# Router logits from x itself, x turned once into the output banks, the norm weight put on at the column copies, and two row products of a pair moved round the turns

## The reference

```python
x = x + m                                     # after the mixer
h = _rmsnorm(x, norm_ffn_g)                   # x * rsqrt(mean(x*x) + EPS) * norm_ffn_g
gp = softmax(ht @ w_router_group)             # 4 groups, the best one is taken
el = (ht @ w_router_expert)[its group]        # 8 experts of it
ep = softmax(el); tv, ti = lax.top_k(ep, 2); tv = tv / sum(tv)
for e in range(32):                           # D_MODEL 1024, EXPERT_FF 512
    a = silu(ht @ w_expert_gate[e]) * (ht @ w_expert_up[e])
    out = out + combine[:, e:e + 1] * (a @ w_expert_down[e])
y = _rmsnorm(x + out, norm_final_g)
```

## Time and profile before

| | us |
|---|---|
| median of 3 runs | 806.62 (805.08 to 806.87) |
| the profiled execution | 806.2 |
| its span | 804.2 |
| PE busy | 773.9 (96%) |
| DVE, ACT, POOL busy | 234.4, 176.4, 97.2 |
| chain that ended last: PE, DMA | 81%, 13% of the span |

### The profile page before, as it was taken

The page is one execution under the profiler, slowest core; times in us unless marked ns, Lnnn a source line. Parts: engine busy times, 40 slices in busy tenths (PEclk is TensorE's granted clock), DMA queues, the critical chain, the costliest instruction groups (busy, mean ns, idle before and its releaser), DMA issues.

```text
span 804.2 us, 10140 instructions
## 1 busy us (share of the span) xinstructions
PE 773.9 (96%) x4170; PEld 445.8 (55%) x4170; DVE 234.4 (29%) x533; ACT 176.4 (22%) x321; POOL 97.2 (12%) x128
## 2 busy tenths in 40 slices
PE   8999999999999999999999999999999989999995
PEld 7888887888888888863333333333333333333331
DVE  4099869482550322441101110111011101101112
ACT  3104333657544101231111001100110010010011
POOL 5300064523300000001101000001000000000001
PEclk9999999999999999999999999999999999999998
DMA  9845586578849974499999999999999999999993
GB/s 329 244 149 187 164 239 207 181 214 169 276 148 365 398 259 191 162 360 430 423 429 417 426 429 425 429 426 427 427 429 427 430 427 429 425 428 419 421 409 149
DMA packets 76374, 267.90 MB, mean 333 GB/s; under 512 B 5598, under 2 KB 37578, under 8 KB 63647
## 3 DMA queue, kind: packets, MB, share of 16 engines
q1 hardware_dynamic: 74402, 264.13, 84.3%
q10 hardware_dynamic: 1461, 1.45, 0.6%
q0 software_dynamic: 464, 1.64, 0.5%
HBM read 259.13 MB, written 8.55 MB: 333 GB/s over the span
## 4 chain that ended last, share of the span: by engine, by line
PE 81%; DMA 13%; DVE 2%; issue 1%; ACT 1%; POOL 1%; SPq 0%; DVEq 0%
PE bank L2007 23%; PE bank L1630 23%; PE bank L2045 10%; PE bank L1903 7%; PE bank L2053 6%; DMA slots<-in_w_expert_gate_dram 5%; DMA x_early<-in_w_expert_gate_dram 5%; DMA slots<-in_w_expert_down_dram 2%; PE bank L1850 2%; PE bank L1740 1%; DMA slots<-in_w_in_dram 1%; PE bank L2034 1%; DVE x_early L1488 1%; PE bank L1971 1%; PE bank L1662 1%
## 5 line engine op out<-in xcount | busy, mean ns | idle before, releaser
L1630 PE MATMUL bank<-hT,slots 128*128 128x264 f32 x832 | 189.6, 387 | 0.0
L2007 PE MATMUL bank<-slots,hT 128*64 128x512 f32 x624 | 177.9, 601 | 2.1 <-DMA slots<-in_w_expert_gate_dram 2.1
L1630 PEld LDWEIGHTS bank<-hT,slots 128*128 128x128 f32 x832 | 156.6, 190 | 26.8 <-issue 0.6
L1488 DVE TENSOR_TENSOR x_early<-x_early,bank 128x512 f32<-128x512 f32 x16 | 11.0, 688 | 376.6 <-PE bank L2007 376.6
L2007 PEld LDWEIGHTS bank<-slots,hT 128*64 128x64 f32 x624 | 55.1, 138 | 91.1 <-issue 86.5
L2045 PE MATMUL bank<-slots,wrep 128*64 128x512 f32 x304 | 85.4, 595 | 4.7 <-ACT wrep L1053 4.0
L2007 PE MATMUL bank<-slot,hT 128*64 128x512 f32 x208 | 81.4, 593 | 0.0
L793 POOL COPY hT<-x_early 128x512 f32 x30 | 17.9, 623 | 369.3 <-PE bank L2007 286.2
L2053 PE MATMUL bank<-hT,diag 128*128 128x512 f32 x128 | 59.2, 605 | 0.2 <-ACT hT L1065 0.2
L2045 PEld LDWEIGHTS bank<-slots,wrep 128*64 128x64 f32 x304 | 26.0, 137 | 49.3 <-issue 39.6
L1228 DVE SCALAR_TENSOR_TENSOR slot<-slot,rows_buf 128x256 f32<-128x256 f32 x120 | 49.4, 488 | 0.0
(11 more groups left out here) (301 smaller groups left out, 759.6 us busy)
## 6 DMA issues: line engine op xcount, KB each, us to landing
slots<-in_w_expert_gate_dram SPq DMA_DIRECT2D x15, 2048.0 KB, 23.2
slots<-in_w_expert_up_dram SPq DMA_DIRECT2D x15, 2048.0 KB, 28.7
slots<-in_w_expert_down_dram SPq DMA_DIRECT2D x15, 2048.0 KB, 29.7
slots<-in_w_in_dram SPq DMA_DIRECT2D x13, 2048.0 KB, 10.0
slots<-in_w_expert_gate_dram SPq DMA_DIRECT2D x10, 1024.0 KB, 26.2
slot<-in_w_expert_gate_dram SPq DMA_DIRECT2D x5, 2048.0 KB, 27.7
slot<-in_w_expert_up_dram SPq DMA_DIRECT2D x5, 2048.0 KB, 23.7
slot<-in_w_expert_down_dram SPq DMA_DIRECT2D x5, 2048.0 KB, 34.1
```

The costliest lines, as they stand in the source:

```text
L1488: dve.tensor_tensor(act.rearrange("s (f c) -> s f c", f=FT), act.rearrange("s (f c) -> s f c", f=FT), bank[UP][:, :].rearrange("s (c f) -> ...
L1630: last = mm(out, w[:, a, t * P:(t + 1) * P], (hT if c else xgain)[:, a, :], start=(a == 0), stop=(a == KT - 1))
L2007: last = mm(out[sl, :], xe[:, a, sl], expert_view(p, kind, e, a // 2)[:, a % 2, :], start=(a == 0), stop=(a == KT - 1))
```

## The change

It has five parts, all after the mixer's last projection but for the first line.

1. **Logits of x.** The router weights are multiplied once by `norm_ffn_g` on DVE, ahead of the wo groups, and `route` reads `xT`. The eight products into `hT` (L1407) are gone, and so are the copy of `hT` to DRAM (`h_rows`, L591) and the waits for it. The branch for experts with over 64 tokens, which this input does not enter, is rewritten to use `tok_rows`.
2. **x turned once.** `seat` now uses the transpose mode, and all four seats stand ahead of the ranking. ACT makes `xrow` from the output banks; only the eight sample rows are still turned into the `misc` banks. The sum of squares is made with 128 moving columns for each token tile, not one.
3. **Norm weight at the copies.** `xrow` now is x times `rs`. The weight is put on where columns are copied: DVE (`first_columns`) makes the first pair's `xe` from the gathered banks, in place of ACT, and POOL multiplies the later pairs' columns by it (L793 was a copy). A small load brings the weight.
4. **The choice** uses the engine's eight-largest operation (`dve.max`) and combined compare-and-multiply operations.
5. **Loads and row products.** SP issues half 18 ahead of `tok_rows`, and 19 ahead of 17. From the fifth pair on, two of the four row products of the pair before leave `combine_prompt` and stand one ahead of `turn(p)` and one behind it; a new semaphore `m_rows` makes ACT's copy to `ytok` and DVE's `weigh` wait for them.

```diff
@@ sync: loads @@
-                if c == WO + 1:
-                    sp.wait_ge(xg_ready, KT)
-                    sp.dma_start(h_rows[:, :, :], hT[:, :, :]).then_inc(h_stored, 16)
                 sp.wait_ge(proj.ready, proj.written(stream[c][1]))
                 load_slot(n)
+                if n == 5:
+                    sp.dma_start(g_by, ins["norm_ffn_g"][0].rearrange("(p a) -> p a", p=P)).then_inc(g_by_in, 16)
             load_half(16)
-            sp.wait_ge(*misc.read(("ht", 5)))
...
-            sp.wait_ge(seated, 1)
+            sp.wait_ge(misc.ready, misc.written(("ht", 5)))
             sp.wait_ge(x_kept, 1)
             load_half(18)
+            sp.wait_ge(row_made, 4)
+            sp.dma_start(tok_rows[0:SEQ, :].rearrange("(t p) d -> p t d", p=P), xrow[:, 0:2, :]).then_inc(rows_kept, 16)
...
@@ gpsimd: columns of pair p @@
-                    pool.tensor_copy(xe[:, :, e * SLOTS:(e + 1) * SLOTS], xall[:, :, bass.ds(at[e], SLOTS)]).then_inc(m_xe, 1)
+                    pool.tensor_tensor(xe[:, :, e * SLOTS:(e + 1) * SLOTS], xall[:, :, bass.ds(at[e], SLOTS)],
+                                       g_by[:, :].unsqueeze(2).broadcast_to([P, KT, SLOTS]), ALU.mult).then_inc(m_xe, 1)
@@ scalar @@
-            second = se.value_load(offs[0:1, 1:2], min_val=0, max_val=SLOTS)
             for j in range(2):
-                se.wait_ge(m_gathered, j + 1)
+                se.wait_ge(first_xe, 2 * j + 2)
...
-                se.copy(xe[:, 4 * j:4 * j + 4, 0:SLOTS], src[:, :, 0:SLOTS]).then_inc(first_xe, 1)
-                se.copy(xe[:, 4 * j:4 * j + 4, SLOTS:], src[:, :, bass.ds(second, SLOTS)]).then_inc(first_xe, 1)
@@ vector @@
+            dve.tensor_tensor(wrout[:, :, :], wrout[:, :, :], vec[:, 60:60 + KT].unsqueeze(2).broadcast_to([P, KT, NG + NE]), ALU.mult).then_inc(router_ready, 1)
...
-                dve.tensor_scalar(hT[:, d, :], xT[:, d, :], vec[:, 60 + d:61 + d], None, ALU.mult).then_inc(xg_ready, 1)
...
+            second = dve.value_load(offs[0:1, 1:2], min_val=0, max_val=SLOTS)
+            dve.wait_ge(g_by_in, 16)
+
+            def first_columns(j):
+                dve.wait_ge(m_gathered, j + 1)
...
+                dve.tensor_tensor(xe[:, 4 * j:4 * j + 4, 0:SLOTS], src[:, :, 0:SLOTS], gain, ALU.mult).then_inc(first_xe, 1)
+                dve.tensor_tensor(xe[:, 4 * j:4 * j + 4, SLOTS:], src[:, :, bass.ds(second, SLOTS)], gain, ALU.mult).then_inc(first_xe, 1)
@@ tensor @@
+            def seat(t, i):
+                for c in range(4):
+                    last = mm(bank[Y_BANKS[t][i]][:, c * P:(c + 1) * P], xT[:, 4 * i + c, t * P:(t + 1) * P], ident[:, :],
+                              start=(c == 0), stop=(c == 3), is_transpose=True)
+                last.then_inc(y_seated, 1)
...
-                last = mm(bank[misc.bank("ms")][0:m, i:i + 1], rstd[:, t0:t0 + m], ones[:, 0:1], start=True, stop=True)
+                last = mm(bank[misc.bank("ms")][0:m, i * P:(i + 1) * P], rstd[:, t0:t0 + m], ones[:, 0:P], start=True, stop=True)
...
-            turn_groups(misc, "ht", hT, beside_rows)
+            for t, i in ((0, 1), (1, 0), (1, 1)):
+                seat(t, i)
...
-            seat(1, 0)
-            seat(1, 1).then_inc(seated, 1)
...
+            def late_rows(p):
+                return p >= len(BLOCKS) - 2
...
                 if 1 < p < PAIRS - 1:
-                    combine_prompt(p - 1)
+                    combine_prompt(p - 1, 2 if late_rows(p - 1) else 4)
                 up(p)
                 if p:
                     combine_samples(p - 1)
+                if p and late_rows(p - 1):
+                    to_rows(p - 1, 1, 0)
                 turn(p)
+                if p and late_rows(p - 1):
+                    to_rows(p - 1, 1, 1).then_inc(m_rows, 1)
```

More of the change, by code:

```diff
@@ L608, in _ @@
             load_half(19)
+            sp.wait_ge(smalls_done, 1)
+            load_half(17)
             load_half(NR)
@@ L763, in _ @@
             pool.memset(dflat[:, T:], 0.0).then_inc(c_const, 1)
-            pool.wait_ge(proj.ready, proj.written(("wo", KT - 1)))
-            pool.wait_ge(xg_ready, KT)
+            pool.wait_ge(*proj.read(("wo", KT - 1)))
             pool.tensor_copy(x_samples, xT[:, :, SEQ:T]).then_inc(x_kept, 1)
@@ L1020, in _ @@
             se.wait_ge(f_rstd, 1)
[L1022 removed]
+            for i in range(4):
                 t, half = i // 2, i % 2
[L1024 to L1028 removed]
+                se.wait_ge(y_seated, i + 1)
+                se.activation(xrow_by[:, t, :, SLOTS * half:SLOTS * half + SLOTS],
+                              bank[Y_BANKS[t][half]][:, :].rearrange("p (q a) -> p a q", a=KT), ACT.Copy,
+                              scale=rs[:, t:t + 1]).then_inc(row_made, 1)
+            for half in range(2):
+                se.wait_ge(misc.ready, misc.written(("ht", 4 + half)))
+                se.activation(xrow_by[0:NB, 2, :, SLOTS * half:SLOTS * half + SLOTS],
+                              bank[misc.bank(("ht", 4 + half))][0:NB, :].rearrange("p (q a) -> p a q", a=KT), ACT.Copy,
+                              scale=rs[0:NB, 2:3]).then_inc(M_act, 1)
             se.wait_ge(exp_in, 1)
@@ L1928, in _ @@
             for i, (t0, m) in enumerate(TOK_TILES):
-                last = mm(bank[misc.bank("ms")][0:m, i:i + 1], rstd[:, t0:t0 + m], ones[:, 0:1], start=True, stop=True)
+                last = mm(bank[misc.bank("ms")][0:m, i * P:(i + 1) * P], rstd[:, t0:t0 + m], ones[:, 0:P], start=True, stop=True)
             last.then_inc(M_ready, 1)
-            def seat(t, i, last=False):
-                for c in range(4):
-                    turned = mm(bank[Y_BANKS[t][i]][:, c * P:(c + 1) * P], xT[:, 4 * i + c, t * P:(t + 1) * P], ident[:, :],
-                                start=(c == 0 and not last), stop=(c == 3 and last))
-                return turned
             def seat_samples(x):
@@ L1941, in seat_samples @@
                        start=False, stop=False, tile_position=(0, at))
-            def beside_rows(t, half):
-                if t and half == 0:
-                    pe.wait_ge(*proj.read(("wo", KT - 1)))
-                    seat(0, t - 1)
-            turn_groups(misc, "ht", hT, beside_rows)
+            for t, i in ((0, 1), (1, 0), (1, 1)):
+                seat(t, i)
+            for half in range(2):
+                misc.before_write(pe, ("ht", 4 + half))
+                out = bank[misc.bank(("ht", 4 + half))]
+                for c in range(4):
+                    last = tr(out[0:NB, c * P:(c + 1) * P], xT[:, 4 * half + c, SEQ:T], ident[:, :])
+                last.then_inc(M_ready, 1)
             pe.wait_ge(member_ready, 1)
@@ L2118, in _ @@
                 pe.wait_ge(y_tok, 5)
-                pe.wait_ge(g_diag, 3)
-                for i, (t0, m) in enumerate(TOK_TILES):
-                    last = mm(bank[4][:, t0:t0 + m], gones[0:m, :], gdiag[0:m, i, 0:m], start=True, stop=True)
-                last.then_inc(g_rms, 1)
+                pe.wait_ge(h_back, 32)
+                for a in range(KT):
+                    if a > 1:
+                        pe.wait_ge(h_ready, a - 1)
+                    for t, (t0, m) in enumerate(TOK_TILES):
+                        last = tr(bank[4 + a % 2][:, t0:t0 + m], gx[0:m, t, a * P:(a + 1) * P], ident[0:m, 0:m])
+                    last.then_inc(g_turned, 1)
                 pe.wait_ge(h_ready, KT)
@@ L2146, in _ @@
                     for i in range(2):
-                        seat(t, i, last=True).then_inc(y_sum, 1)
+                        for c in range(4):
+                            last = mm(bank[Y_BANKS[t][i]][:, c * P:(c + 1) * P], xT[:, 4 * i + c, t * P:(t + 1) * P], ident[:, :],
+                                      start=False, stop=(c == 3))
+                        last.then_inc(y_sum, 1)
                 mm(bank[GATE][:, 0:PART], ident[:, :], sample_sum, start=True, stop=False)
```

117 lines of the change are left out of this document (62 added, 55 removed).

## The result

| | before | changed |
|---|---|---|
| median, 12 runs each (us) | 805.85 | 809.42 |
| lowest to highest (us) | 805.08 to 806.87 | 806.25 to 810.55 |
| ratio to before, 95% interval | | 1.0036 [1.0027, 1.0045] |
| span of the profiled execution (us) | 804.2 | 808.6 |

What follows compares the result with a forecast made beforehand. The landing of the last weights was taken as the bound, moving with the first load after a DMA hole. Span 804.2, 2.0 around it, 0.4 up to the median and 0.0 from that load gave 806.6 us, range 804.8 to 808.6.

Steps and rivals of the forecast that it cites:

- The bound: Late pairs: the last weight to land sets the end, so the end moves with the first load after the hole.
- the first load after the hole: Weight load ending the DMA dip from 344 us; half 19 replaces 17, forecast at 349.6 against 349.53, no change, chance 0.48.
- Logits, choice, ranking: Routing stage: logits 0.4 us earlier, choice gains 1.1, ranking starts at 337.0 to 338.5, `first_block` taken at 341.8.
- The gap: Before `first_block`: PE's idle time grows from 0.73 to 2.7 us; a clock fall costs 0 to 2.1 us, taken 1.6.
- Full clock in `first_block`: Rival: no clock fall follows the idle gap; 804.2 to 805.7 us, middle 805.2; chance 0.25.
- the copy of `xrow`: Copy to `tok_rows` ahead of half 19: lands at 346 to 347, not the last to come.
- Half clock through the stage: Rival: routing stage's turns do not bring the clock back; 808.1 to 809.4 us, middle 808.6; chance 0.14.
- DVE's load of the register: First pair's columns: 0.66 us, fitting into the 3.1 us until the first bank is gathered; cost 0.
- POOL's multiply: Later pairs' columns: 1.26 us against the copy's 0.62, 1.3 more a pair; 0 to 1.3 of PE at pair 1.
- The waits round the turn: PE's 0.29 and 0.68 us idle go, up to 0.97 in each of 12 pairs; the weights' landing takes it all.
- The base: Starting level: 804.2 us of span, 2.0 around it, 0.4 up to the median.

Runs made afterwards that it cites:

- e11: Changed kernel with eight 512-column products, read by nobody, between the idle gap and `first_block`; 813.80 us, ratio 1.0102.
- e2: Changed kernel with 16 filler turns (transposes of the identity) between ranking and `first_block`; 804.35 us, ratio 0.9980.
- e5: e2 with SP's two copies of `xrow` to `tok_rows` issued ahead of half 18; 804.41 us, ratio 0.9981.
- e1: Changed kernel with 16 filler products of the identity with itself between ranking and `first_block`; 805.44 us, ratio 1.0000.
- e6: e2 with 8 filler turns instead of 16; 804.80 us, ratio 0.9989.
- e7: Kernel before the change, with only the move of the row products added; 806.10 us, ratio 1.0010.
- e8: Changed kernel with SP's two copies of `xrow` issued ahead of half 18, without filler; 807.94 us, ratio 1.0028.
- e4: Changed kernel with the row products back, all four of a pair behind `gate`; 807.04 us, ratio 1.0030.
- e3: Kernel before the change, with 16 seat products put ahead of the ranking, leaving PE idle before `first_block`; 809.83 us, ratio 1.0065.
- e10: e5 with the row products back behind `gate` in the last pair alone; 804.22 us, ratio 0.9985.

## Why the prediction was wrong

The forecast was no change, 806.6 in 804.8 to 808.6; the measured median is 809.42.

- **The bound, right.** The end moved with the first load after the hole: 3.6 us later there, 4.3 at the last quarter; from the change to e11 it is 3.8 us more there and 3.5 in the span. It holds for losses, and to about a microsecond. Gains beyond e2 no longer reached the end (e5); e1 and e2 have half 19 within 0.15 us and spans of 804.0 and 802.7; and in six profiles (e1, e2, e6, e7, e8, e11) PE did not wait for any quarter of the last `down`.
- **Logits, choice, ranking, right.** The choice began 1.44 us after the start of the last add where it took 1.83 (0.4 taken), and took from 333.28 to 337.29, 4.0 us for 5.0 (1.1 taken). The ranking started at 337.34 (337.0 to 338.5), `first_block` at 341.59 (341.8 taken), after 2.78 us of idle time (2.7 taken). Two small misses cancel in the 341.8: I had the ranking at 337.9, and counted 3.9 us from it to `first_block`, from the end of the turns at 340.62, though the ranking had begun at 340.45; it took 4.25.
- **The gap, the step that failed.** Its mechanism was in the text and its price was not. I took the cost of a fall from the earlier trace rows, where `gate` with its 512 columns lost 2.1 us, and let that be the upper end: 0 to 2.1, taken 1.6. In the profile `first_block` lost 5.3 us, for the clock stood low for 17.1 us, where the fall in that `gate` lasted 3.4; in e8 and e4 it lost 4.1 and 3.2. With 5.3 in place of 1.6 the sum gives 353.3 for the first load (353.13 measured) and 810.3, which is the profiled execution's own 810.4. The row from which I took the price had another kind of work behind the idle time, and I used its end as a bound where no reason made it one. The whole of `first_block` stood at 0.50 in the profile, and 5.3 us is what that costs, 0.46 us for each microsecond at the low clock; e8 and e4, with 8.8 and 7.8 us of `first_block` before the clock came back, 6.8 of them low in e4, fit this price. So the end of the term's range would have had to be 5.3. The `gate(0)` behind it lost 1.7 us more to the same fall:

```profile
352.99 8.76 PE L2028 MATMUL bank<-slots,hT 128*64 128x512 f32 x32
```

Why the fall lasted so long, and differently from run to run, stays open.
- **Full clock in `first_block`** was a rival at 805.2 with a chance of 0.25. No execution of the changed kernel is seen to have it: e4's profile, a low one by its span of 804.9, has a fall of 6.8 us, and the four low runs of the change have mean granted clocks of 0.990 to 0.993, where those of e2 that its ratio counts have 0.994 to 0.998. So the group at 806.3 is more likely one of shorter falls. What full clock gives is shown by e2 and e6, 804.35 and 804.80. The price was near, though its first load was not: I had the copy of `xrow` landed at 346 to 347, and e1, e2 and e6 issue half 19 at 348.9 to 349.1, held by its receipt. It now stands behind half 18 on SP's queue. The working was wrong too: 12.7 us from 332 on give 344.7, not 346 to 347, and the rate was not 414 GB/s throughout but 274 in 332 to 336 and 322 in 340 to 344 of the changed kernel.
- **Half clock through the stage** gave the nearest time (808.6), by the wrong cause: the clock was at 1.00 until 339.3, though PE did nothing but turns from 334.4 to 336.8, and the 16 turns of e2 held it up. So the Trainium skill's rule (TensorE: Matmul & The Clock Gate, Part 4: PE-mode transpose), that transposes do not count as a busy PE, does not describe this stage; as a filler, products and turns did the same. The fall of the kernel before at 334.8 did come among turns, but e3 and e7 have the same turns there and no fall.
- **Smaller terms.** DVE's load of the register stood for 1.89 us, not 0.66, and was hidden all the same. POOL's multiply takes 1051 ns for 1264 and was never waited for, at pair 1 either (0 to 1.3 given). The waits round the turn went and came back as waits for weights, as forecast. Below are PE's waits from 364 us on (line, releaser: us in total, times, longest), two of the kernel before and then two of the changed one.
```profile
PE bank L2045 <- ACT wrep L1053: 8.3, 13, 0.7
PE bank L2034 <- DVE x_early L1488: 4.9, 15, 0.9
```

```profile
PE bank L2055 <- DVE x_early L1512: 1.4, 3, 0.9
PE bank L2066 <- ACT wrep L1059: 0.7, 1, 0.7
```

- **The base.** I added 0.4 us from the profiled execution to the median of three runs; the median of twelve is 0.4 below it, 805.85. That execution had a fall of the clock at 334.8 to 338.2 which e7, with the same stage, does not have, and e7's first load goes at 348.40, 1.1 us earlier: the level to beat was probably lower than its profile said (argued, since e7's own span, with its falls and its second hole, is 804.5).

## What to carry to other kernels

An idle time of TensorE in front of a chain of short products is a cost of its own, with a spread from run to run: price it by the whole of the work that follows at the low clock (here 11.47 us for 6.17), not by a fall seen ahead of other work, and look whether the change takes away what used to fill it. Filling the gap with work that nobody reads (16 turns of the identity, 2 us) turned 0.36% slower into 0.20% faster here; a filler that outlasted the gap (e1) gave back part of it. And when an early step is made faster, follow every transfer that its new order puts behind a load, since its receipt may be next.

## What the runs showed of the hardware

**How long a fall lasted.** The falls of the clock to 0.50 lasted about 3.4 us (twelve of them: one among the turns ahead of the ranking, 334.8 to 338.2 in the kernel before, five behind the one-column products, and six in the late pairs; those in the last 10 us of the kernel are left out), 6.8 (e4, e11), 10.2 (e8) and 17.1 us (the changed kernel), with the same instructions in and behind the gap in e4, e8 and the change.

**After what idle time.** At the gap, none of the nine profiles with 0 to 1.8 us of idle time has a fall between the ranking and the end of `first_block`; of the five with 2.7 to 2.8 us four have one, and they began 0.5 to 3.8 us after the ranking had ended. With 1.76 us of idle time none of ten runs was above 806.7. PE's waits in the expert stage, in all fourteen profiles, say the same: behind 49 waits of 1.3 to 1.8 us there is no fall, and of seven waits of 1.98 to 2.89 us six have one behind them, within 1.4 us of PE's start. So in these profiles the falls behind idle time stand behind 1.98 us of it and more, mostly but not always (2.04 us in the changed kernel and 2.71 in e3 had none).

**With PE busy.** Behind the 24 products of one column (2.73 us) a fall began in five of thirteen profiles (e1, e2, e7, e10, e11), 0.2 to 0.9 us after their end, though PE was busy throughout.
